# One GpSimd copy of 1024 columns in place of two of 512 in the weight split of a two-layer hybrid encoder

## What is computed

```python
h = _rmsnorm(x, norm_g)
z = h @ w_in                       # even layer, 1024 -> 5648
aq, ak, av, bq, bk, bv, blr, gate = _split(z, SPLIT_EVEN)
...                                # A: attention over 64-frame chunks, B: gated linear attention, 4 heads
y = jnp.concatenate([ao.astype(x.dtype), bo], axis=-1) * jax.nn.silu(gate)
return x + y @ w_out, new_k, new_v, s_new
...
xb, gate = _split(h @ w_in, (C_WIDTH, C_WIDTH))   # odd layer: conv, two block-diagonal gates, scan
y = hs.astype(x.dtype) * jax.nn.silu(gate)
return x + y @ w_out, new_conv, hs[:, -1]
```

## Time and profile before

| | us |
|---|---|
| three runs | 1538.31, 1535.05, 1535.10 |
| median | 1535.10 |
| profiled execution, whole | 1536.87 |
| its span, first to last instruction | 1535.0 |
| PE busy | 1505.5 |
| POOL busy | 517.3 |
| DVE busy | 846.2 |

### The profile page before, as it was taken

One profiled execution on the slowest core, in us unless ns is written; L12 is line 12 of the kernel. 1 busy time (PEld: TensorE's weight loads), 2 busy tenths in 40 slices (PEclk: granted clock), 3 DMA queues, 4 the chain that ended last, 5 costly groups with the idle time before them and its releaser, 6 DMA issues.

```text
span 1535.0 us, 24191 instructions
## 1 busy us (share of the span) xinstructions
PE 1505.5 (98%) x9622; PEld 1418.6 (92%) x9622; DVE 846.2 (55%) x1411; ACT 454.7 (30%) x808; POOL 517.3 (34%) x466
## 2 busy tenths in 40 slices
PE   7999999999989999999999999999999999999997
PEld 7998878887779999999999999999999999999996
DVE  6115767777874633646257111377686776784113
ACT  5112333343453132131142000215335152461002
POOL 5142111111102321223224323335454453545433
PEclk9999999999999999999999999999999999999998
DMA  5221010100001111111101333111111111122223
GB/s 202 79 63 58 18 42 28 45 29 29 15 20 37 42 45 35 32 34 41 45 35 57 114 100 100 65 48 56 56 54 57 42 56 50 51 83 85 85 84 117
DMA packets 29350, 89.39 MB, mean 58 GB/s; under 512 B 3600, under 2 KB 8784, under 8 KB 29264
## 3 DMA queue, kind: packets, MB, share of 16 engines
q1 hardware_dynamic: 19632, 64.27, 12.8%
q10 hardware_dynamic: 9632, 23.91, 4.8%
HBM read 76.64 MB, written 11.67 MB: 58 GB/s over the span
## 4 chain that ended last, share of the span: by engine, by line
PE 93%; DVE 4%; issue 1%; DMA 1%; ACT 1%; ACTq 0%; POOL 0%; DVEq 0%; POOLq 0%
PE ps L386 60%; PE ps L551 10%; PE ps L431 8%; PE ps L491 2%; PE ps L507 2%; PE ps L520 2%; PE ps L715 1%; PE ps L636 1%; PE ps L620 1%; PE ps L631 1%; PE ps L610 1%; DVE arena L1293 1%; PE ps L530 1%; DVE Yr L1402 1%; DVE arena L1265 1%
## 5 line engine op out<-in xcount | busy, mean ns | idle before, releaser
L386 PE MATMUL ps<-H,w_hi 128*128 128x364 f32 x2796 | 566.8, 330 | 10.1 <-ACT H L825 7.7
L351 POOL CAST w_hi<-raw 128x512 fp32r<-128x512 f32 x226 | 185.6, 821 | 974.1 <-PE ps L386 594.6
L386 PEld LDWEIGHTS ps<-H,w_hi 128*128 128x128 f32 x2796 | 479.1, 189 | 12.5 <-issue 11.0
L386 PE MATMUL ps<-H,w_lo 128*128 128x364 f32 x1716 | 379.2, 329 | 0.0
L353 POOL TENSOR_TENSOR w_lo<-raw,w_hi 128x512 fp32r<-128x512 f32 x226 | 324.2, 1435 | 18.1
L386 PEld LDWEIGHTS ps<-H,w_lo 128*128 128x128 f32 x1716 | 299.6, 189 | 0.0
L551 PE MATMUL ps<-H,w_hi 128*128 128x364 f32 x672 | 145.0, 338 | 1.0 <-DVE arena L1238 1.0
L386 PE MATMUL ps<-Yr,w_hi 128*128 128x364 f32 x636 | 141.2, 330 | 0.9 <-DVE Yr L1590 0.9
L916 ACT ACTIVATE arena<-arena,sm 128x256 f32<-128x256 f32 (+1 forms) x144 | 69.6, 485 | 211.0 <-DVE sm L1278 211.0
L431 PE MATMUL ps<-w_hi,H 128*128 128x256 f32 (+1 forms) x720 | 129.8, 282 | 1.3 <-ACT Y L875 0.7
L1539 DVE TENSOR_TENSOR arena<-ps,arena 128x1092 f32 (+1 forms) x15 | 19.4, 1295 | 197.8 <-PE ps L386 197.8
(11 more groups left out here) (199 smaller groups left out, 1813.9 us busy)
## 6 DMA issues: line engine op xcount, KB each, us to landing
raw<-weights SPq DMA_DIRECT2D x113, 512.0 KB, 3.5
arena<-xT ACTq DMA_DIRECT2D x15, 546.0 KB, 5.3
x_scratch<-arena ACTq DMA_DIRECT2D x8, 546.0 KB, 6.0
arena<-x_scratch ACTq DMA_DIRECT2D x8, 546.0 KB, 3.7
arena<-k_scratch ACTq DMA_DIRECT2D x8, 304.0 KB, 4.1
yT<-arena SPq DMA_DIRECT2D x2, 768.0 KB, 4.4
yT<-arena SPq DMA_DIRECT2D x2, 576.0 KB, 3.2
k_scratch<-Y ACTq DMA_DIRECT2D x2, 512.0 KB, 2.8
```

Source lines behind the costliest of these rows:

```text
L351: pool.tensor_copy(w_hi[:, s, cols], raw[:, s, cols]).then_inc(w_hi_done, 1)
L386: mm = pe.matmul(sets[st][:, c, 0:CW], lw[:, s, w], rx[:, k, c * CW:(c + 1) * CW], start=(first and n == 0 and m == 0), stop=(last and n = ...
```

## The change

POOL copies the whole piece at once, 128 x 1024, after a wait for `piece_done` of piece p-2, and then subtracts in two halves as before, each raising `w_split`. `w_hi_done` counts once for a piece. `half_done` is raised by PE as before, and POOL no longer waits for it.

```diff
             def split(i, s, first):
                 pool.wait_ge(w_in[s], 16 * i + 16)
+                if not first:
+                    pool.wait_ge(piece_done, 2 * i + (s - 1))
+                pool.tensor_copy(w_hi[:, s, :], raw[:, s, :]).then_inc(w_hi_done, 1)
+                pool.wait_ge(w_hi_done, 2 * i + (s + 1))
                 for h in range(2):
                     cols = slice(h * HALF, (h + 1) * HALF)
-                    if not first:
-                        pool.wait_ge((half_done, piece_done)[h], 2 * i + (s - 1))
-                    pool.tensor_copy(w_hi[:, s, cols], raw[:, s, cols]).then_inc(w_hi_done, 1)
-                    pool.wait_ge(w_hi_done, 4 * i + (2 * s + h + 1))
                     pool.tensor_tensor(w_lo[:, s, cols], raw[:, s, cols], w_hi[:, s, cols].bitcast(F32),
                                        ALU.subtract).then_inc(w_split, 1)
```

## The result

The changed kernel takes 1551.57 us (median of four, 1551.13 to 1552.81) against 1535.07 before: slower by a ratio of 1.0099, 95% interval 1.0086 to 1.0111. The forecast was 1542.5, the range ended at 1547.0. The direction was right and the size less than half: 7.35 us were forecast, 16.5 lie between the medians (15.2 by the ratio).

What follows compares the result with a forecast made beforehand. PE was taken as the bound, busy 1505.5 of 1535.0 us. Late splits, 5.5 (heads) + 0.7 (piece 4) + 1.15 (piece 5) = 7.35 us, took the median from 1535.1 to 1542.5; range 1538 to 1547.

Steps and rivals of the forecast that it cites:

- PE as the bound, GpSimd's total counting for nothing: Whole kernel: PE busy 1505.5 of 1535.0 us; GpSimd's saving of 11 us is off PE's path and counts as nothing.
- The copy, 1.13 us: Each 1024-column GpSimd copy: 2 x 614 - 93 = 1135 ns, bounded by 1.05 and 1.23 us.
- The five late splits, 7.35 us: Value projections of heads 1 to 3, 5.5 us; piece 4, 0.7; piece 5, 1.15: PE waits for late second or first halves.
- the absorption: Piece 4, first value projection: 1.57 us late, 0.86 absorbed by PE's existing wait for ACT, 0.7 stays.
- rival A: At the late pieces DVE does not come between the two subtractions; 3.8 us slower in all, 1538.9; chance 0.2.
- Where that is hidden: Step asking where PE's matmuls cover the later splits: 12.0 us a piece, 6.0 in the odd layer; three kinds of places left.
- The attention has more cover still: Attention: more matmul cover than the 6.0 us elsewhere, so no loss was counted there.
- the paragraph on the heads: Value projections of heads 1 to 3: second halves late by 1.97, 1.74 and 1.74 us with DVE between subtractions; sum 5.5.
- rival C: Relief: fewer GpSimd operations free DVE, giving back 4.3 of PE's 14.0 us of waits; not slower; chance 0.05.
- Rival B, turns that cost more: GpSimd and DVE taking turns costs more, making piece 48 in the even projection 1.9 us late; 9 to 11.4 us; chance 0.15.
- the same pattern: Odd projection taken to behave as the even one, where pairs taken in turns count 0, range 0 to 1.9 us.

Runs made afterwards that it cites:

- attention_only: Whole-piece copy only at pieces 9 to 22, read during the attention, all others split as in the kernel before; ratio 1.0026 to it, 4.0 us slower.
- Five_only: Whole-piece copy only at pieces 4, 5, 30, 36 and 42, others as in the kernel before; ratio 1.0038 to it, 5.8 us slower.
- turns_apart: Kernel before with whole-piece copy only at pieces 62, 63, 98, 99, their second subtraction waiting for half_done; ratio 1.0011 to it, 1.7 us slower.

## Why the prediction was wrong

**PE as the bound, GpSimd's total counting for nothing:** right. The forecast had 11 us less of copying, 56 came, and they brought nothing that can be seen.

**The copy, 1.13 us:** it took 1.04, the lower bound of 1.05. I had taken the fixed part from the subtraction, 93 ns; the two copies give it directly, 2 x 614 - 1041 = 187 ns. The slope is (1041 - 614) / 512 = 0.83 ns a column. The Trainium skill (GPSIMD Engine Reference, "3.1 Elementwise — side-by-side cycle accounting") gives 1.03 cycles an element for a loop body of at most two operations. With the 1.2 GHz of its "1. Specifications" that is an estimate of 0.86 ns a column; the 0.83 measured agrees with it and not with the 1.02 that I used.

**The five late splits, 7.35 us:** right in place, to the piece, and near in size; how the second half comes late in the heads was wrong. PE's rows of the changed kernel:

```profile
54.33 0.38 PE L430 MATMUL ps<-w_hi,H 128*128 128x256 f32 x1 [0.88 <-POOL w_lo L353]
...
55.57 0.39 PE L430 MATMUL ps<-w_hi,H 128*128 128x256 f32 x1 [0.27 <-POOL w_lo L353]
...
79.06 0.74 PE L385 MATMUL ps<-H,w_hi 128*128 128x364 f32 x3 [1.27 <-POOL w_lo L353]
...
646.32 0.38 PE L430 MATMUL ps<-w_hi,H 128*128 128x256 f32 x1 [0.68 <-POOL w_lo L353]
647.57 0.39 PE L430 MATMUL ps<-w_hi,H 128*128 128x256 f32 x1 [0.27 <-POOL w_lo L353]
```

Measured in lag: 0.85 at piece 4 (0.7 forecast, with the absorption), 1.0 at piece 5 (1.15, from terms that sum to 1.17), and 1.6, 1.5 and 1.5 in the heads (1.97, 1.74, 1.74). That is 6.5 us; alone these five pieces cost 5.8. The forecast let one DVE operation in between the two subtractions. Head 1, GpSimd with the two subtractions shown one by one, then DVE:

```profile
545.35 1.17 POOL L349 CAST w_hi<-raw 128x1024 fp32r<-128x1024 f32 x1 [5.81 <-PE ps L385]
546.59 2.20 POOL L353 TENSOR_TENSOR w_lo<-raw,w_hi 128x512 fp32r<-128x512 f32 x1
548.75 1.28 POOL L353 TENSOR_TENSOR w_lo<-raw,w_hi 128x512 fp32r<-128x512 f32 x1
```
```profile
545.65 2.01 DVE L1372 TENSOR_TENSOR arena<-arena 128x1088 f32<-128x1088 f32 x1
...
548.90 2.27 DVE L1372 TENSOR_TENSOR arena<-arena 128x1088 f32<-128x1088 f32 x1
```

The L1372 of 545.65 was already waiting when the copy ended at 546.52, and it went in ahead of the first subtraction, which took 2.20 us. The next L1372 came at 548.90, when the second subtraction had run since 548.75, and was itself held; the second took 1.28. Piece 4 and the other two heads read the same, with 2.20 to 2.40 and then 1.28 or 1.29. So the two subtractions did stand back to back, as rival A had it, and yet A's 3.8 us were too few, since the operation came in one step earlier. The pair takes about as long either way, 3.43 us against 1.29 + 2.22, so that the forecast's number came near is in part luck. The rest of the difference is the copy: cheaper by 0.09 us, and it waited beside DVE for 0.13 us in head 1 and not at all in the other two, in place of 0.40 and 0.17.

Rival A's premise, that GpSimd holds what it has from one subtraction to the next, is not a rule either. At piece 98 an operation of DVE was already waiting (Yr, from 1384.52) when the first subtraction ended, and the second took 2.34 us:

```profile
1385.70 2.34 POOL L353 TENSOR_TENSOR w_lo<-raw,w_hi 128x512 fp32r<-128x512 f32 x1
```

**The step that failed** is "Where that is hidden", with the words "The attention has more cover still". It put the attention at nothing by one question, whether a split comes in time for PE. That part was right: none was late there. It never asked what GpSimd's longer run does to the other engine that shares its way into SBUF, and whether PE waits for that engine. What stood there in place of nothing is the attention's 4.0 us, measured alone (5.3 by the lag), and 3.4 at the two turns of stage. The first half of the question could be answered before: the earlier trace rows show DVE operations held by a subtraction, and the paragraph on the heads prices the reverse, GpSimd held by DVE. I used the turns only where a split was already late. Where I did name VectorE's side, in rival C, I gave it the wrong sign, a relief, and wrote that few or no splits run in the attention, where there are fourteen. The rival's bound, PE's 14.0 us of waits, bounds a gain; a loss has no such bound.

**Rival B, turns that cost more:** near in kind, wrong in place. It looked at piece 48. There PE's lag stays where it was; at the odd output projection, which I waved through as "the same pattern", and at the odd layer's start, which I judged by its cover alone, 3.0 and 1.6 us arose. The range, built from A and B, did not reach the result, since the attention was in neither.

**The clock, and what stays open.** A part of the losses at the turns is not waiting. Behind the waits of the changed kernel PE ran for some microseconds at a lower granted clock. Stretches of the changed kernel (PE busy, PEld, DVE, ACT, POOL, PEclk, DMA share, GB/s):

```profile
1008.00:1014.00 6.00, 5.64 (x41) 5.34 (x40) 4.70 (x8) 2.59 (x4) 1.74 (x1) 1.00 0.39 129
1014.00:1018.00 4.00, 4.00 (x15) 3.76 (x14) 2.31 (x3) 0.00 (x0) 0.00 (x0) 0.57 0.00 0
...
1393.00:1397.00 4.00, 4.00 (x17) 4.00 (x16) 4.00 (x4) 3.98 (x5) 0.00 (x0) 0.58 0.65 257
```

Of the kernel before, around the same matmuls:

```profile
998.00:1006.00 8.00, 8.00 (x51) 7.26 (x50) 5.29 (x9) 2.38 (x4) 2.29 (x2) 1.00 0.28 87
1370.00:1377.00 7.00, 5.88 (x24) 5.48 (x24) 7.00 (x9) 6.97 (x8) 1.15 (x1) 0.76 0.21 75
```

The clock has two levels, 1.2 and 2.4 GHz, and 0.57 over such a stretch is mostly the lower. What PE did ahead of them: in the odd layer it waited 0.4 us, in the output projection 2.9 us for DVE's Yr, and then worked without a gap. By the lag each stretch costs 1.4 to 1.5 us. At the odd layer's start that is nearly all of the 1.6. At the output projection PE waited 3.4 us for Yr in all, against 0.9 before. But the kernel before had a slow stretch of its own just ahead of the second of these waits, which made PE late and the wait short; it cost nothing in the end, since attention_only, without one, is 5.6 us behind ahead of the place and 5.65 behind it. Five_only and attention_only, which split by halves there, waited 2.2 us. So the turn adds 1.2 us of waiting, which fits the 1.1 that L1650 was held, and its slow stretch 1.5: nearly all of the 3.0.

At the two turns the slow stretch goes with the change. Of the fourteen profiles, the three with the long copy and joined subtractions at pieces 62 and 63 have one at the odd layer's start and the other eleven none. Behind the last wait for Yr, the seven with any changed split at pieces 98 and 99 have one, after a wait of 1.8 to 2.9 us, and the other seven none, with waits of at most 1.4. In the attention and near 777 us (by the time line of the kernel before) the stretches move: seven profiles have one near 777, neither the kernel before nor the changed one among them, and it costs each 1.5 us. So single profiles mislead by as much as the effects sought. The executions of the kernel before, timed beside turns_apart, run from 1534.78 us at a mean clock of 0.996 to 1540.21 at 0.993. How much of each measured ratio is clock was not separated, and what makes a stretch fall in the attention in one execution and not in the next stays open.

## What to carry to other kernels

When an edit on one engine joins short operations to a longer unbroken run, ask two questions and not one: who waits for the results, and who shares the path to memory during the run. The second is answered by laying the run's new start and end over the other engine's time line at each recurring step: here a run of 3.6 in place of 2.0 us met a two-column operation 2.7 us in. Where such a run has slack, break it with a wait for an event that comes later anyway; that recovered all of the attention's loss. And count nothing for fewer, larger operations on an engine that is not the bound: here 56 us less of GpSimd's time brought nothing.

## What the runs showed of the hardware

An operation of two columns on VectorE that reads SBUF twice was held 0.6 to 1.06 us by one GpSimd subtraction of 512 columns, up to as long as L1650 with its 1024 columns (2.30 in place of 1.21 us). The Trainium skill (SBUF — State Buffer, "SBUF: two separate sides") says that the shared pair is an exclusive lock held for the whole instruction; the trace agrees: 149.32 + 0.93 = 150.25, and the subtractions end at 147.71 + 2.53 = 150.24. What I had not expected is that a narrow operation is held as long as a wide one, so that the cheapest operations of a chain lose the most by proportion. Who goes first was decided by who was already waiting: a VectorE operation that waited when a GpSimd instruction ended got in before the next one, behind a copy (the 2.20 us of 546.59) and between two subtractions (the 2.34 of 1385.70) alike; one that came 0.15 us after the next had started was held for the rest of it (the 2.27 of 548.90). A GpSimd copy of float32 to fp32r costs 0.19 us and 0.83 ns a column.
